# Next stage's first weights made a block earlier, one-tile lag and a single sum of squares at three norm-and-add passages

## What is computed

```python
def rmsnorm_2(x, w):
    xf = x.astype(jnp.float32)
    y = xf * lax.rsqrt(jnp.mean(xf * xf, axis=-1, keepdims=True) + EPS)
    return (y * w.astype(jnp.float32)).astype(x.dtype)
...
    for layer in range(DEPTH_2):
        h = rmsnorm_2(x, norm_mix_pre[layer])
...
        x = x + rmsnorm_2(y, norm_mix_post[layer])
        h = rmsnorm_2(x, norm_ffn_pre[layer])
        y = conv_ffn(h, ffn_w_up[layer], ffn_conv_w[layer], ffn_conv_b[layer], ffn_w_down[layer])
        x = x + rmsnorm_2(y, norm_ffn_post[layer])
        if layer == N_A_LAYERS - 1:
            k_sh, v_sh, c_sh = shared_kv(x, kv_norm, kv_w, kv_b_f)
```

## Time and profile before

| | us |
|---|---|
| median of 3 runs | 2117.31 |
| lowest and highest | 2116.98, 2117.67 |
| profiled execution, span | 2113.2 |
| TensorE busy | 2056.7 (97%) |
| VectorE busy | 1221.0 (58%) |
| ScalarE busy | 792.2 (37%) |

### The profile page before, as it was taken

One profiled execution on the slowest core, in us unless ns is written; L12 is line 12 of the kernel. 1 busy time (PEld: TensorE's weight loads), 2 busy tenths in 40 slices (PEclk: granted clock), 3 DMA queues, 4 the chain that ended last, 5 costly groups with the idle time before them and its releaser, 6 DMA issues.

```text
span 2113.2 us, 25707 instructions
## 1 busy us (share of the span) xinstructions
PE 2056.7 (97%) x9944; PEld 1667.1 (79%) x9944; DVE 1221.0 (58%) x1717; ACT 792.2 (37%) x1231; POOL 24.4 (1%) x45
## 2 busy tenths in 40 slices
PE   8999999999999999999999999999999999999997
PEld 6866778888888888777788888878786678888886
DVE  5778635554435355556675573763537756647475
ACT  4258243332212232345443342442427734324242
POOL 1000000000000000000000000000000000000000
PEclk9999999999999999999999999999999999999998
DMA  5410412322222222321122222222220022222221
GB/s 186 163 40 10 145 37 100 110 99 100 100 99 87 94 100 90 109 91 60 60 100 100 100 80 103 82 95 90 99 88 33 21 80 80 100 100 99 95 85 59
DMA packets 34320, 188.52 MB, mean 89 GB/s; under 512 B 4392, under 2 KB 8648, under 8 KB 14608
## 3 DMA queue, kind: packets, MB, share of 16 engines
q1 hardware_dynamic: 32448, 181.24, 24.1%
q0 software_dynamic: 1568, 5.65, 1.0%
q10 hardware_dynamic: 208, 0.33, 0.1%
HBM read 182.54 MB, written 2.11 MB: 87 GB/s over the span
## 4 chain that ended last, share of the span: by engine, by line
PE 90%; DVE 4%; PEld 3%; issue 1%; ACT 1%; DVEq 1%; PEldq 0%; DMA 0%; SPq 0%; ACTq 0%
PE bank L411 23%; PE bank L413 23%; PE bank L412 23%; PE bank L492 4%; PE bank L497 4%; PE bank L493 4%; PE bank L1212 2%; PE bank L1242 2%; PE bank L1229 2%; PE bank L653 1%; DVE w_lo L359 1%; PEld bank L411 1%; PEld bank L413 1%; PEld bank L412 1%; PE bank L2250 1%
## 5 line engine op out<-in xcount | busy, mean ns | idle before, releaser
L345 ACT ACTIVATE w_hi<-w_raw 128x2048 fp32r<-128x2048 f32 (+3 forms) x174 | 314.1, 1805 | 771.4 <-PE bank L413 633.0
L411 PE MATMUL bank<-a_hi,w_hi 128*128 128x512 f32 x1376 | 539.2, 392 | 4.3 <-DVE shared L2610 1.6
L413 PE MATMUL bank<-a_hi,w_lo 128*128 128x512 f32 x1376 | 535.7, 389 | 0.0
L412 PE MATMUL bank<-a_lo,w_hi 128*128 128x512 f32 x1376 | 535.5, 389 | 0.0
L359 DVE TENSOR_TENSOR w_lo<-w_raw,w_hi 128x2048 fp32r<-128x2048 f32 (+3 forms) x174 | 374.9, 2157 | 167.2 <-ACT w_hi L345 167.2
L411 PEld LDWEIGHTS bank<-a_hi,w_hi 128*128 128x128 f32 x1376 | 258.3, 188 | 60.8 <-issue 4.3
L413 PEld LDWEIGHTS bank<-a_hi,w_lo 128*128 128x128 f32 x1376 | 258.2, 188 | 54.0
L412 PEld LDWEIGHTS bank<-a_lo,w_hi 128*128 128x128 f32 x1376 | 258.4, 188 | 53.0
L411 PE MATMUL bank<-big_halves,w_hi 128*128 128x512 f32 x616 | 240.1, 390 | 0.5 <-DVE w_lo L359 0.3
L412 PE MATMUL bank<-big_halves,w_hi 128*128 128x512 f32 x616 | 239.7, 389 | 0.0
L413 PE MATMUL bank<-big_halves,w_lo 128*128 128x512 f32 x616 | 239.7, 389 | 0.0
(11 more groups left out here) (342 smaller groups left out, 2373.4 us busy)
## 6 DMA issues: line engine op xcount, KB each, us to landing
w_raw<-in_w_fu SPq DMA_DIRECT2D x44, 1024.0 KB, 4.8
w_raw<-in_w_up SPq DMA_DIRECT2D x16, 1024.0 KB, 4.8
w_raw<-in_w_down SPq DMA_DIRECT2D x16, 1024.0 KB, 4.8
w_raw<-in_w_fd SPq DMA_DIRECT2D x16, 1024.0 KB, 4.8
w_raw<-in_w_fd SPq DMA_DIRECT2D x8, 768.0 KB, 4.2
w_raw<-in_w_rqk SPq DMA_DIRECT2D x4, 1024.0 KB, 5.3
w_raw<-in_w_rvg SPq DMA_DIRECT2D x4, 1024.0 KB, 5.0
w_raw<-in_w_gate SPq DMA_DIRECT2D x4, 1024.0 KB, 4.8
```

What stands on the lines that cost most here:

```text
L345: act.activation(w_hi[slot][:, cols], raw[slot][:, cols], ACT.Copy).then_inc(hi_half_ready.sem if half == 0 else hi_ready.sem, 1)
L411: pe.matmul(out, w[0], x[0], start=first, stop=False)
L412: pe.matmul(out, w[0], x[1], start=False, stop=False)
L413: return pe.matmul(out, w[1], x[0], start=False, stop=last)
```

## The change

- A stage that ends in a passage is "eager": behind the late piece of its block 1 the parts of the next stage's block 0 are made, into a third pair of weight buffers (`spare_w`, a part of `big_halves3` that is free at these times); in its block 2, where block 0's parts were made, those of the next stage's block 1. The two rings of buffers swap their turn after each such stage. The two halves inside the passage are gone. Block 2's parts in the next stage wait only for the products of the stage before.
- VectorE scales y in place, two tiles ahead, adds it to x, and adds up all squares of the new x into `total`; each square has a buffer of its own (`square_of`). TensorE has one group of column sums, behind step 5.
- Block 1 runs one tile behind block 0 (`lag=1`), not three.

```diff
+        stream = {"slot": 0, "turn": 0}
+        spare_w = [big_halves[3][:, n * SLOT:(n + 1) * SLOT] for n in range(2)]
+
+        def ring_of(spec, nxt, b, slot, m):
+            if isinstance(b, int) and b == (spec.blocks if m["eager"] else 0) and (m["eager"] or m["crossed"]):
+                return spare_w
+            turn = 1 if m["eager"] and isinstance(b, int) and b > spec.blocks else 0
+            return [x[(slot + m["turn"] + turn) % 2] for x in (w_hi, w_lo)]
...
         def hi_part(act, spec, nxt, b, q, m, half=None):
...
-            act.wait_ge(products_done.sem, m["prod"] + b - 1)
+            if dst is not spare_w:
+                early = isinstance(b, int) and (b == spec.blocks + 1 or (m["crossed"] and b == 2))
+                act.wait_ge(products_done.sem, m["prod"] + b - (2 if early else 1))
...
             for b in range(first, n):
                 early(eng, b, slot(b % 2), m)
-                if n > 1 and b + 2 <= n and not (lag and b == 0):
+                if m["eager"] and b == 2:
+                    part(eng, spec, nxt, 5, 1, m)
+                elif n > 1 and b + 2 <= n and not (lag and b == 0):
                     part(eng, spec, nxt, b + 2, b % 2, m)
                 late(eng, b, slot(b % 2), m)
+                if m["eager"] and b == 1:
+                    part(eng, spec, nxt, 4, 0, m)
...
             def ahead_act(act, part):
-                part(0)
                 act_post(act)
-                part(1)
                 for k in range(KT):
                     act.wait_ge(updated.sem, b_up + k + 1)
                     high(act, k, pre)
-                    square(act, k)
+                    if k >= 5:
+                        act.wait_ge(gathered.sem, b_ga + k - 4)
+                    act.activation(square_of(k), xT[:, k, :], ACT.Square).then_inc(squared.sem, 1)
                 part(None, 2)
                 act_root(act)
...
             def ahead_dve(dve, part):
-                def weights():
-                    part(0)
-                    part(1)
-                dve_post(dve, weights)
+                dve_post(dve, lambda: None)
+                scale(dve, 0)
+                scale(dve, 1)
+                add(dve, 0)
                 for k in range(KT):
-                    scale_tile(dve, src, vec, k, b_sc, b_up)
-                    if k >= 1:
-                        dve.wait_ge(updated.sem, b_up + k)
-                        low(dve, k - 1, pre, b_hi)
-                    add_tile(dve, k, b_sc)
-                    if k >= 6:
-                        gather(dve, k - 2)
-                dve.wait_ge(updated.sem, b_up + KT)
-                low(dve, KT - 1, pre, b_hi)
-                gather(dve, 6)
+                    if k + 2 < KT:
+                        scale(dve, k + 2)
+                    low(dve, k, pre, b_hi)
+                    if k + 1 < KT:
+                        add(dve, k + 1)
+                    if k >= 2:
+                        gather(dve, k - 1)
+                gather(dve, KT - 1)
                 part(None, 2)
                 dve_root(dve)
...
             def with_tile(pe, k):
-                if 1 <= k <= 3:
...
-                elif k == KT:
...
-                elif k == KT + 1:
+                if k == 5:
+                    pe.wait_ge(gathered.sem, b_ga + KT - 1)
+                    column_sums(pe, 4, total, True, True).then_inc(sums_ready.sem, 1)
+                elif k == 6:
                     pe_root(pe)
```

More of the change, by code:

```diff
@@ L327, in hi_part @@
         def hi_part(act, spec, nxt, b, q, m, half=None):
-            beyond = isinstance(b, int) and b == spec.blocks
+            beyond = isinstance(b, int) and b >= spec.blocks
             if beyond and nxt is None:
@@ L341, in hi_part @@
             act.wait_ge(raw_loaded[slot].sem, before + 16 * turn)
-            act.wait_ge(products_done.sem, m["prod"] + b - 1)
+            if dst is not spare_w:
+                early = isinstance(b, int) and (b == spec.blocks + 1 or (m["crossed"] and b == 2))
+                act.wait_ge(products_done.sem, m["prod"] + b - (2 if early else 1))
             cols = columns_of(n, half)
-            act.activation(w_hi[slot][:, cols], raw[slot][:, cols], ACT.Copy).then_inc(hi_half_ready.sem if half == 0 else hi_ready.sem, 1)
+            act.activation(dst[0][:, cols], raw[slot][:, cols], ACT.Copy).then_inc(hi_half_ready.sem if half == 0 else hi_ready.sem, 1)
         def lo_part(dve, spec, nxt, b, q, m, half=None):
-            beyond = isinstance(b, int) and b == spec.blocks
+            beyond = isinstance(b, int) and b >= spec.blocks
             if beyond and nxt is None:
@@ L479, in begin, with weights, tile @@
                     pe.wait_ge(evacuated.sem, m["evac"] + b - 1)
[L480 to L485, removed]
+                    slot = (m["slot"] + q) % 2
+                    return slot, [x[(slot + m["turn"]) % 2] for x in (w_hi, w_lo)], chunks[q % len(chunks)]
+                def weights(ring, col):
+                    return [x[:, col:col + P] for x in ring]
+                def tile(b, slot, ring, sets, k):
                     high_in, low_in = tile_ready(k)
@@ L496, in tile @@
                         col, x = sets[c][k]
-                        last = pe.matmul(bank[2 * slot + c][:, :], weights(slot, col)[0], x[1], start=False, stop=final)
+                        last = pe.matmul(bank[2 * slot + c][:, :], weights(ring, col)[0], x[1], start=False, stop=final)
                         if final and b == 1 and c == 0 and len(sets) > 1:
@@ L504, in by_tile @@
                     first = begin(0, 0, halved)
-                    tiles = len(first[1][0])
+                    if lag:
+                        first = first[0], spare_w, first[2]
+                    tiles = len(first[2][0])
                     for k in range(tiles + (lag or 0)):
@@ L518, in by_chunk @@
                 def by_chunk(b, q, first=False):
-                    slot, sets = begin(b, q)
+                    slot, ring, sets = begin(b, q)
                     n = 0
@@ L525, in by_chunk @@
                             col, x = sets[c][k]
-                            last = three_products(pe, bank[2 * slot + c][:, :], weights(slot, col), x, k == 0, k == len(sets[c]) - 1)
+                            last = three_products(pe, bank[2 * slot + c][:, :], weights(ring, col), x, k == 0, k == len(sets[c]) - 1)
                             n += 1
@@ L894, in ahead_dve, with gather, add @@
+            def gather(dve, k):
+                dve.wait_ge(squared.sem, b_sq + k + 1)
+                if k > 1:
+                    dve.wait_ge(gathered.sem, b_ga + k - 1)
+                dve.tensor_tensor(total[:, :], total[:, :], square_of(k), ALU.add).then_inc(gathered.sem, 1)
+            def add(dve, k):
+                dve.wait_ge(scaled.sem, b_sc + k + 1)
+                dve.tensor_tensor(xT[:, k, :], xT[:, k, :], src[:, k, :], ALU.add).then_inc(updated.sem, 1)
             def ahead_dve(dve, part):
-                def weights():
-                    part(0)
-                    part(1)
@@ L907, in ahead_dve @@
-                dve.wait_ge(updated.sem, b_up + KT)
-                low(dve, KT - 1, pre, b_hi)
-                gather(dve, 6)
+                    if k + 2 < KT:
[6 more added lines that the diff above has]
+                gather(dve, KT - 1)
                 part(None, 2)
                 dve_root(dve)
-            def sums(pe, src, first, last):
-                column_sums(pe, 4, src, first, last).then_inc(sums_ready.sem if last else summed.sem, 1)
```

61 lines of the change are left out of this document (20 added, 41 removed).

## The result

The changed kernel takes 2106.18 us (median of 4 runs, 2105.42 to 2106.41) against 2117.49 (4 runs); the ratio is 0.9946, 95% interval 0.9934 to 0.9958. Forecast: 2107.1, range 2104.0 to 2112.0. Run once more in a later group: 2106.15 (5 runs, 2104.23 to 2107.57). The profiled execution of the changed kernel took 2106.26, with a span of 2104.5.

A forecast was written before the change was run, and what follows sets the result against it. TensorE was taken to bound the kernel, busy 97% of the span, with VectorE's new order pacing the passages up to the sums. Savings of 3.5, 3.2 and 3.5 us, together 10.2, took 2117.3 to 2107.1 us; range 2104 to 2112.

The forecast's parts named there:

- The sum: Three passages (layer output normalised, added to x, handed to next projection): 3.5, 3.2, 3.5 us saved, 10.2 together.
- rival 2: The new wait at the sums lowers TensorE's clock; 1.6 to 1.7 us lost a passage, 2112; chance 0.11, shared with longer VectorE chain.
- VectorE sets the pace, TensorE waits for it: In the pair of blocks, VectorE's last addition ends at t0 + 21.33; TensorE waits for it before the sums.
- t0: Zero of each passage's times: the moment VectorE can use the spread root; block 2 forecast at t0 + 29.8.
- rival 1: TensorE, not VectorE, sets the pace and the wait at the sums goes: 3 x 1.9 us more, 2101.4; chance 0.03.
- The wait: TensorE, before the single group of column sums, waits 1.9 us for VectorE's last addition, to t0 + 21.38.
- The low clock after the restart: TensorE's first 3.39 us after the restart at t0 + 2.91 run at 1.2 GHz and hold eight matmuls.
- The additions: VectorE's adding up of the new x's squares, four extra additions of 0.60 us a passage, done at t0 + 21.33.
- What lies around the span: Outside the profiled span of 2113.2 us: 4.1 us up to the median of 2117.3, taken as untouched.
- Rival 3: The low clock lasts through the pair: 12 us a passage slower, 36 in all, 2153; chance 0.05 with the like.
- Rival 4: Moved weights delay the stage before's last evacuation or block 3; 0 to 1 us kept a passage; 0.09 with rival 5.
- Rival 5: The change does not do what it says; only the weight halves' cover could fail; chance 0.09 with rival 4.

The follow-up runs named there:

- sums_earlier: Changed kernel with the column sums and the root's spread one step earlier (sums behind 54 of 96 matmuls); 2124.43 us, ratio 1.0027 to before.
- fill_after: Changed kernel with TensorE's idle time around the spread filled by products that nobody reads; 2107.69 us, ratio 0.9952 to before.
- sums_later: Changed kernel with the column sums and the root's spread one step later (sums behind 78 of 96 matmuls); 2105.57 us, ratio 0.9938 to before.
- squares_only: Kernel before with only the squares' part: squares added on VectorE, one sums group, old weights and three-tile distance; 2110.42 us, ratio 0.9959 to before.
- lag2: Changed kernel with block 1 two tiles behind block 0, sums behind step 6, spread behind step 7; 2107.17 us, ratio 0.9941 to before.
- after_again: The changed kernel unaltered, run again in a later group; 2106.15 us (5 runs), ratio 0.9935 to before.
- lag2_first: lag2 with the first add to x ahead of the second scale; 2106.23 us (6 runs), ratio 0.9929 to before.

## Why the prediction was right

*The sum.* Forecast were 3.5, 3.2 and 3.5 us a passage. The two traces of the changed kernel give 1.80, 3.08, 3.35 and 3.41, 3.08, 3.38. The difference is the fall in passage 1, which rival 2 had priced at 1.6 to 1.7. That the time came within 1 us of the forecast is in part luck: of the 10.2 us forecast, the passages of these traces give 8.2 and 9.9, the spans differ by 8.7 and 8.8, and the medians by 11.3. The steps below say where these part.

*VectorE sets the pace, TensorE waits for it.* Right, and shown from both sides: the sums stand at t0 + 21.16 whether TensorE comes at 16.7 to 17.8 (sums_earlier), at 18.9 (fill_after) or at 19.5 to 20.4 (changed). So rival 1 is out. The Trainium skill, "VectorE: DVE Perf Modes", section "Rules for kernel authors", had spoken against chained additions. The trace agrees that they are not free, but 0.8 to 1.7 of the 3.24 us that they save TensorE came back as this wait, not the 2.4 that the prediction worked out by the rule.

*Terms mis-sized.* The wait: 1.9 forecast, 0.81, 1.09 and 1.68 measured. The low clock after the restart was taken as 3.4 us; it lasted 2.9, 4.8 and 4.2 in passages 1 to 3, so TensorE came to the sums at t0 + 19.5, 20.35 and 20.1 against 19.45. The later coming in passages 2 and 3 cost nothing, the wait absorbed it; passage 1, with the shortest low clock, had the longest wait, and behind it the clock fell. The additions ended 0.2 earlier than walked, the rest took 8.73 (29.89 - 21.16) and not 8.42; the two cancel.

*t0 is no common zero.* It lies behind the spread, which takes 1.16 us at the full clock and up to 2.08 where the clock has fallen. The first trace of the changed kernel spends 1.2 us more in its three spreads than before's. From the spread's start the passages gained 1.38, 3.26 and 2.43, 7.1 in all, and the spans differ by 8.7; where the other 1.6 came from was not traced. The code ahead of the spread doesn't decide how long it takes: sums_later, with the changed kernel's code there, has 1.16 three times, and squares_only, with before's, has 2.08 twice.

*What lies around the span.* This step was wrong and did no harm to the forecast. I took 4.1 us (2117.3 - 2113.2) as time outside the span that stays. In the changed kernel's runs time and span differ by 1.8, in the 40 later runs of before by 1.8 to 3.3. The result is 2113.2 - 8.7 + 1.8 and the forecast was 2113.2 - 10.2 + 4.1: 1.5 us less came off, 2.3 less came on top, and the two errors largely cancel. The traced execution of before was an unusual one, as the view of the cores shows: its mean clock was 0.993,

```profile
core 0: 2113.2 us, clock 0.993
```

higher than in any of those 40 runs. Of the 29 in the first two later groups two had 0.992 (2116.0 us in the mean), nine 0.991 (2117.2), nine 0.990 (2118.5), one 0.989 (2120.6) and eight 0.988 (2121.9). With the differences above, a span of 2113.2 goes with a time of 2115.0 to 2116.5, under each of the three times in the median; which execution was traced is not on record.

*The other rivals.* Rival 3: no gap follows the restart in the changed kernel, and the lift comes after 2.9 to 4.8 us. Rival 4: the rows of fd02 above, and in both traces of the changed kernel TensorE waits for no weights in the 60 us behind the start of block 2. Rival 5: the parts did what they say.

## What to carry over

Where one engine hands over to another, place the hand-over by a walk through both queues, and then look at what is left behind it: one step too early cost 18 us here, one step too late is bound by the next evacuation, and by the passages the right place came with one more tile of distance. A kernel whose clock falls at a few places should be compared by a distance inside the trace that excludes the others; lag2's whole time hid a gain of 3.3 to 4.9 us. A single profiled span may belong to an unusual execution: before it is subtracted from a median, its mean clock is to be compared with that of the other runs. Products without a reader in short pauses shortened the passages (2.8 us in one trace) where TensorE's pace counted, and not where another engine set it.

## What the runs showed of the hardware

*Pauses and the clock.* Inside the pair the full clock survived waits of 0.81 to 1.16 us (five of them in the two traces of the changed kernel). Behind a wait of 1.68, and within or behind those of 3.3 to 4.4, it fell; of three waits of 2.26 to 2.29 it fell behind two. The length of the pause alone doesn't decide it. The Trainium skill, "TensorE: Matmul & The Clock Gate", section "Part 1: The HAM clock gate", has the low level as what an idle engine falls back to; the traces agree, and add that a single wait between full products can be enough (1.68 us in passage 1 of the changed kernel), though it isn't always (2.26 us in passage 2 of fill_after).

*The same code, two clocks.* In the first block 64 products of 64x32 stand between dense products. First the changed kernel, then lag2, the same instructions:

```profile
95.61 3.76 PE L1495 MATMUL bank<-shared,big 64*128 64x32 f32 x64
99.30 0.50 PE L427 MATMUL bank<-a_hi,w_hi 128*128 128x512 f32 x1
99.64 0.39 PE L428 MATMUL bank<-a_lo,w_hi 128*128 128x512 f32 x1
```

```profile
96.77 4.54 PE L1495 MATMUL bank<-shared,big 64*128 64x32 f32 x64
101.24 0.79 PE L427 MATMUL bank<-a_hi,w_hi 128*128 128x512 f32 x1
101.83 0.63 PE L428 MATMUL bank<-a_lo,w_hi 128*128 128x512 f32 x1
```

TensorE hardly pauses there, yet in lag2 the clock fell during the small products (the stretch from 100 to 110 has 0.68). It fell again near 144 (0.70 from 140 to 150), where TensorE does pause: it is busy 3.55 of the 5 us from 140. All five runs of lag2 had a mean clock of 0.987 to 0.989, all five of sums_later, on the same chip in the same group, 0.991 or 0.992.

Yet the kernel alone doesn't decide it. The two traces of the changed kernel differ at 144 us, first trace and after_again (PEclk is the third number from the end):

```profile
140.00:150.00 10.00, 8.19 (x67) 5.39 (x68) 9.61 (x29) 8.95 (x33) 0.00 (x0) 1.00 0.01 2
```

```profile
140.00:150.00 10.00, 8.32 (x60) 5.83 (x61) 9.31 (x28) 8.31 (x30) 0.00 (x0) 0.83 0.01 2
```

In the trace of sums_later the clock falls near 100 and near 141, too, for half as long as in lag2, and six runs of lag2_first on one chip go from 0.986 to 0.992. What decides it from one execution to the next, and why lag2's five runs agree so well, stays open.
